# Trailing means moved to GpSimd, decayed values taken from PSUM, and another order of fills in a triangular inverse

## What is computed

```
x = x + 0.5 * swiglu(rms(x));  h = rms(x);  proj = h @ w_in            # 3080 columns
aq, ak, av, pu, dq, dk, dv, dz, db, da = split(proj)
ya = dilated_attention(rope(aq), rope(ak), av)       # 4 heads x 64
yb = pool_w_g( mean of the last w positions of pu_g - pu_g ) * scale   # w = 2, 4, 8, 16; 4 groups x 64
yc = rms(delta_rule(q, k, v, decay, beta)) * silu(dz)  # 4 heads x 128, after a causal conv of 4 taps
x = x + concat(ya, yb, yc) @ w_out;  x = x + 0.5 * swiglu(rms(x))
```

## Time and profile before

| what | value |
|---|---|
| three runs, median | 1019.83 us |
| profiled execution, its own time | 1020.79 us |
| its span, first to last instruction | 1019.0 us |
| granted TensorE clock, mean | 0.998 |
| mixer of layer 0, inverse up to the new values | 264.5 to 288.4 us |

### The profile page before, as it was taken

How to read it: one execution, slowest core, us unless ns; L and a number is a source line. 1 busy time by engine, 2 the same in 40 slices (tenths; PEclk the granted TensorE clock), 3 DMA queues, 4 the chain that set the end, 5 groups by cost and what they waited for, 6 DMA issues and landing times.

```text
span 1019.0 us, 19068 instructions
## 1 busy us (share of the span) xinstructions
PE 1007.4 (99%) x6482; PEld 883.7 (87%) x6482; DVE 726.7 (71%) x1204; ACT 602.6 (59%) x1101; POOL 235.7 (23%) x248
## 2 busy tenths in 40 slices
PE   9999999999999999999999999999999999999996
PEld 7888888899988888888888888889999888888885
DVE  5787666899777866666786666668986877666666
ACT  6555555777665655555675555558675575555554
POOL 2767222100400122222202222220014002222221
PEclk9999999999999999999999999999999999999999
DMA  7966666485224666666637666656832238666651
GB/s 232 285 209 200 190 194 192 126 242 160 75 64 124 189 206 191 195 188 187 205 123 226 188 191 193 191 157 169 228 110 64 87 101 269 196 190 190 189 182 41
DMA packets 249882, 176.79 MB, mean 173 GB/s; under 512 B 5876, under 2 KB 235401, under 8 KB 249705
## 3 DMA queue, kind: packets, MB, share of 16 engines
q1 hardware_dynamic: 248800, 174.35, 56.7%
q0 software_dynamic: 400, 1.43, 0.4%
q10 hardware_dynamic: 632, 0.34, 0.1%
HBM read 175.05 MB, written 1.05 MB: 173 GB/s over the span
## 4 chain that ended last, share of the span: by engine, by line
PE 92%; DVE 5%; ACT 2%; issue 0%; DVEq 0%; POOL 0%; POOLq 0%; ACTq 0%
PE bank L768 26%; PE bank L772 14%; PE bank L739 13%; PE bank L740 13%; PE bank L741 13%; PE bank L755 3%; PE bank L758 1%; PE bank L779 1%; DVE Wl L1887 1%; PE bank L1169 1%; PE bank L1156 1%; PE bank L1092 1%; ACT X L1491 0%; DVE X L1929 0%; PE bank L814 0%
## 5 line engine op out<-in xcount | busy, mean ns | idle before, releaser
L1887 DVE TENSOR_TENSOR Wl<-raw,Wh 128x1024 fp32r<-128x1024 f32 x324 | 401.7, 1263 | 52.9 <-ACT Wh L1420 52.7
L1420 ACT ACTIVATE Wh<-raw 128x1024 fp32r<-128x1024 f32 x323 | 322.1, 1047 | 20.7 <-PE bank L741 18.3
L768 PE MATMUL bank<-X,Wh 128*128 128x512 f32 x1216 | 288.3, 389 | 0.0
L768 PEld LDWEIGHTS bank<-X,Wh 128*128 128x128 f32 x1216 | 228.0, 188 | 47.2
L622 POOL TENSOR_TENSOR gact<-gact,pooled 128x256 f32<-128x256 f32 x85 | 63.6, 748 | 569.2 <-DVE gact L1986 559.7
L772 PEld LDWEIGHTS bank<-X,Wl 128*128 128x128 f32 x1216 | 153.9, 189 | 5.8
L772 PE MATMUL bank<-X,Wl 128*128 128x256 f32 x1216 | 155.8, 281 | 0.0
L739 PE MATMUL bank<-Wh,aH 128*128 128x512 f32 x336 | 132.4, 394 | 0.2
L740 PE MATMUL bank<-Wl,aH 128*128 128x512 f32 x336 | 131.8, 392 | 0.0
L741 PE MATMUL bank<-Wh,aL 128*128 128x512 f32 x336 | 130.8, 389 | 0.0
L1552 ACT ACTIVATE aH<-hid 128x256 fp32r<-128x256 f32 x84 | 35.1, 418 | 148.8 <-DVE hid L2001 148.8
(11 more groups left out here) (319 smaller groups left out, 1371.3 us busy)
## 6 DMA issues: line engine op xcount, KB each, us to landing
raw<-in_ffn_w_gate SPq DMA_DIRECT2D x88, 512.0 KB, 4.6
raw<-in_ffn_w_up SPq DMA_DIRECT2D x88, 512.0 KB, 3.9
raw<-in_ffn_w_down SPq DMA_DIRECT2D x88, 512.0 KB, 3.4
raw<-in_w_in SPq DMA_DIRECT2D x48, 512.0 KB, 4.9
raw<-in_w_out SPq DMA_DIRECT2D x16, 512.0 KB, 3.6
cst<-in_consts POOLq DMA_DIRECT2D x1, 1200.0 KB, 6.4
xr<-in_x SPq DMA_DIRECT2D x2, 512.0 KB, 4.1
out_x<-big SPq DMA_DIRECT2D x3, 256.0 KB, 2.6
```

The costliest lines, as they stand in the source:

```text
L768: nc.tensor.matmul(b[:, :], piece(Wh, 3 * par + j)[:, k, :], X[:, k, :, :], start=k == 0, stop=False)
L1420: return nc.scalar.activation(Wh[:, s, 0:D_MODEL], raw[:, s, :], ACT.Copy).then_inc(hi_cast.sem, 1)
L1887: return nc.vector.tensor_tensor(low_at(s, skewed), raw[:, s, :], Wh[:, s, 0:D_MODEL].bitcast(F32), ALU.subtract).then_inc(lo_cast.sem, 1)
```

## The change

1. Pieces 21, 22, 23 become: second pool block, fourth gate block, first pool block. Each is made with channels on partitions, by `fill(first, last)`, which runs steps of these three pieces; 24 steps as before, in five groups with ends 4, 9, 14, 19, 24.
2. The four groups of pool products and the two copies of their result go. ScalarE copies each pool block from PSUM to `win_x` (`pool_raw`), and GpSimd adds shifted copies of it, seven instructions for block 1 and five for block 0, each waiting for the one before it. The constant table is 688 KB in place of 1200 KB.
3. The turns of V come after level 0, in PSUM banks 0 and 1, the turns of q and k within the half level.
4. The half level's P for c = 1 and D for c = 0 are interleaved, one product of each in turn.
5. `Vd` is formed from PSUM with beta times decay ahead of `Vn`.
6. On VectorE the copies to `DT` move ahead of the half level's negations. On ScalarE the copies of V come after level 0, and the table load after the fourth gate block's activation, which moves behind the edges.

TensorE's order after the change:

```diff
+                fill(0, FILL_ENDS[0])
                 for n in range(len(LEVELS)):
-                    fill = z_part if n < Z_LEVELS else (lambda ks: att_late(6, ks))
-                    k = 4 * (n % 2)
                     for stage in (level_p, level_d):
                         for c in range(HALVES):
                             stage(n, c)
-                    fill(range(k, k + 4))
-                for first, second, k in ((quarter_p, quarter_d, 0), (half_p, half_d, 4)):
-                    for stage in (first, second):
-                        for c in range(HALVES):
-                            stage(c)
-                    att_late(7, range(k, k + 4))
-                turn_qk()
+                    if n == 0:
+                        turn_v()
+                    else:
+                        fill(FILL_ENDS[n - 1], FILL_ENDS[n])
+                for stage in (quarter_p, quarter_d):
+                    for c in range(HALVES):
+                        stage(c)
+                fill(FILL_ENDS[3], FILL_ENDS[4])
+                half_level()
...
+                def half_level():
+                    pe.wait_ge(*d_done.at(layer, 8 + 1))
+                    for h, u in units(0):
+                        m = half_p(h, u)
                     m.then_inc(p_done.sem, 1)
+                    turn_qk(0)
+                    pe.wait_ge(*d_done.at(layer, 8 + 2))
+                    pe.wait_ge(*pm_done.at(layer, 10 + 1))
+                    pe.wait_ge(*dt_edge.at(layer, 1))
+                    for (h, u), (_, v) in zip(units(0), units(1)):
+                        p = half_p(h, v)
+                        d = half_d(h, u)
+                    p.then_inc(p_done.sem, 1)
+                    d.then_inc(dd_done.sem, 1)
+                    turn_qk(1)
+                    pe.wait_ge(*pm_done.at(layer, 10 + 2))
+                    pe.wait_ge(*dt_edge.at(layer, 2))
+                    for h, u in units(1):
+                        m = half_d(h, u)
+                    m.then_inc(dd_done.sem, 1)
...
-                pe.wait_ge(*pool_copied.at(layer, 2))
+                pe.wait_ge(*win_step.at(layer, 12))
+                pe.wait_ge(*z_act.at(layer, 4))
```

GpSimd, after the rotary products:

```diff
+                def window(op):
+                    win_count[0] += 1
+                    op.then_inc(win_step.sem, 1)
+                    pool.wait_ge(*win_step.at(layer, win_count[0]))
+                def windows(j):
+                    pool.wait_ge(*pool_x.at(layer, 2 - j))
+                    x, lower, upper = win_x[:, j, 1:], slice(0, POOL_DIM), slice(POOL_DIM, P)
+                    a, b = win_a[:, 8:], win_b[:, 4:]
+                    share = cst[:, C_POOL + j * SEQ:C_POOL + (j + 1) * SEQ]
+                    window(nc.gpsimd.tensor_tensor(a, x, win_x[:, j, 0:SEQ], ALU.add))
+                    rows = upper if j == 0 else slice(0, P)
+                    window(nc.gpsimd.tensor_tensor(b[rows, :], a[rows, :], win_a[rows, 6:6 + SEQ], ALU.add))
+                    if j == 1:
+                        window(nc.gpsimd.tensor_tensor(a, b, win_b[:, 0:SEQ], ALU.add))
+                        window(nc.gpsimd.tensor_tensor(b[upper, :], a[upper, :], win_a[upper, 0:SEQ], ALU.add))
+                    window(nc.gpsimd.tensor_tensor(pooled[lower, j, :], a[lower, :], share[lower, :], ALU.mult))
+                    window(nc.gpsimd.tensor_tensor(pooled[upper, j, :], b[upper, :], share[upper, :], ALU.mult))
+                    window(nc.gpsimd.tensor_tensor(pooled[:, j, :], pooled[:, j, :], x, ALU.subtract))
...
+                windows(1)
+                windows(0)
                 ffn(layer, 1)
```

VectorE:

```diff
-                for c in range(HALVES):
-                    dve.wait_ge(*p_done.at(layer, 10 + c + 1))
-                    nc.vector.tensor_scalar(PM[HALF:, 4 * c:4 * c + 4, 0:HALF],
-                                            bank[4 + c][HALF:, 0:4 * HALF].rearrange("p (u t) -> p u t", u=4), -1.0, None,
-                                            ALU.mult).then_inc(pm_done.sem, 1)
                 dve.wait_ge(*cleared.at(layer, 1))
                 for c in range(HALVES):
                     u = slice(4 * c, 4 * c + 4)
                     dve.wait_ge(*dt_edge.at(layer, c + 1))
                     for q in BLOCKS:
                         op = nc.vector.tensor_copy(DT[q, u, q], T64[q, u, :])
                     op.then_inc(dt_joined.sem, 1)
+                for c in range(HALVES):
+                    dve.wait_ge(*p_done.at(layer, 10 + c + 1))
+                    nc.vector.tensor_scalar(PM[HALF:, 4 * c:4 * c + 4, 0:HALF], ...
                 lo_mix(layer, 26)
                 lo_mix(layer, 27)
...
+                small(nc.vector.tensor_tensor(beta_dec, beta_k[:, 0:4], dec[:, 0:4, P - 1:P].rearrange("p u t -> p (u t)"),
+                                              ALU.mult))
+                dve.wait_ge(*vn_ps.at(layer, 1))
+                nc.vector.tensor_tensor(Vd, bank[4][:, :].rearrange("p (u d) -> p u d", u=4),
+                                        beta_dec.unsqueeze(2).broadcast_to([P, 4, P]), ALU.mult).then_inc(vd_done.sem, 1)
                 new_values(0)
-                dve.wait_ge(*vn_done.at(layer, 1))
-                nc.vector.tensor_tensor(Vd, Vn[:, 0:4, :], dec[:, 0:4, P - 1:P].broadcast_to([P, 4, P]),
-                                        ALU.mult).then_inc(vd_done.sem, 1)
```

More of the change, by code:

```diff
@@ L1106, in mixer, with turn_qk @@
                 pe.wait_ge(*at_done.at(layer, 4))
-                def turn_qk():
+                def turn_qk(j):
                     pe.wait_ge(*roped.at(layer, 4))
-                    for j in range(2):
-                        for c in range(HALVES):
[L1113 to L1124, removed]
-                                  k == 0, k == KT - 1)
[L1126 to L1140, removed]
+                    pe.wait_ge(*v_copied.at(layer, j + 1))
@@ new lines, in turn_qk, with fill @@
+                    for c in range(HALVES):
+                        for pair in range(2):
+                            m = nc.tensor.transpose(bank[j][:, pair * SEQ + c * P:pair * SEQ + (c + 1) * P],
+                                                    qkr[:, c, j * 256 + pair * P:j * 256 + (pair + 1) * P], ident)
+                    m.then_inc(qk_turned.sem, 1)
+                def fill(first, last):
+                    for step in range(first, last):
+                        n, k = divmod(step, KT)
+                        pos, out = FILL_POSITIONS[n], bank[(3, 2, 3)[n]][:, 0:SEQ]
+                        s = MIX_SLOTS[pos]
+                        if step == first or k == 0:
+                            split(pos)
+                            if pos == POS_POOL1:
+                                pe.wait_ge(*diff_done.at(layer, 2))
+                            elif pos == POS_Z3:
+                                pe.wait_ge(*z_act.at(layer, 3))
+                            else:
+                                pe.wait_ge(*pool_x.at(layer, 1))
+                        m = three(out, piece(Wh, s)[:, k, :], low_piece(s)[:, k, :], Xh[:, k, :], Xl[:, k, :],
+                                  k == 0, k == KT - 1)
+                        if k == KT - 1:
+                            m.then_inc(proj.sem, 1)
@@ L1195, in quarter_d, with half_p @@
                     m.then_inc(dd_done.sem, 1)
[L1197 to L1202, removed]
-                    m.then_inc(p_done.sem, 1)
[L1205 to L1211, removed]
+                def half_p(h, u):
+                    return nc.tensor.matmul(bank[4 + u // DN_HEADS][HALF:, h * HALF:(h + 1) * HALF], LT[0:HALF, u, HALF:],
+                                            D64[0:HALF, u, :], start=True, stop=True)
@@ L1817, in mixer @@
                                      ACT.Copy).then_inc(o_done.sem, 1)
-                for j in range(2):
-                    act.wait_ge(*pool_ps.at(layer, j + 1))
-                    nc.scalar.activation(pooled[:, j, :], bank[2 + j][:, 0:SEQ], ACT.Copy).then_inc(pool_copied.sem, 1)
                 out_stats(0)
```

144 lines of the change are left out of this document (70 added, 74 removed).

## The result

The changed kernel takes 1021.66 us (median of 20 executions), the kernel before 1020.08 in the same rounds: a ratio of 1.0017, 95% interval 1.0011 to 1.0023. It is slower by 1.6 us, clear of the noise and just under 0.2%. The forecast was 1023.2 us, +3.4; sign and mechanism held, the size was about half. (One slow execution of the 20 took more than twice the time of the rest; medians and ratio don't hang on it.)

A forecast was written before the change was run, and what follows sets the result against it. TensorE, busy 1007.4 of 1019.0 us, was taken as the bound. State product +1.7 us per layer, twice, is 3.4: 1020.79 becomes 1024.2, or 1023.2 against the median 1019.83; range 1017.3 to 1024.5 (8 in 10).

The forecast's parts named there:

- timetable without GpSimd: Both mixers, inverse to state product, nothing held by GpSimd: state product at 290.45 against 291.73, -1.28 us per layer.
- The mechanism of the forecast: Inverse's end to Vd: VectorE's copies, casts and small product take turns with GpSimd's windows; state product +1.7 us per layer.
- C: The forecast itself: copies and casts held by GpSimd's windows, state product late, 1022.0 to 1024.3 us; chance 0.50.
- rival B: Half level to Vd: casts held but not copies; -0.3 to +0.2 us per layer, 1019.6 to 1020.2; chance 0.22.
- Rival A: Half level to Vd: VectorE and GpSimd hardly hold each other; -1.28 us per layer, 1017.3, or 1017.0; chance 0.20.
- D: Besides C, windows reach past 299 and the pooled product waits: 1 to 3 us per layer, 1025 to 1029; chance 0.08.
- the lower bound: State product's delay if the casts catch the gaps in GpSimd's work: +1.1 us per layer, where +1.7 was forecast.
- the wide range that reaches into A: Whole kernel's time, for 8 chances in 10: 1017.3 to 1024.5 us.
- the band "within": Whole kernel, a change under the measurable 0.2% (2.0 us): rival B and what of A and C falls short; chance 0.27.

## Why the prediction was right, and where its size was off

**TensorE's own work: right.** The timetable without GpSimd (-1.28 a layer, 1017.3) was measured as 1017.41 without windows. The inverse's levels take 4.07, the pair 0.61 (0.55 forecast).

**The mechanism of the forecast: right.** VectorE's two-input casts, the small product and the copies are held beside GpSimd. Of the copies no row of before spoke; they take 2.14 for 1.21, and 2.59 in the kernel before with windows added. This was the point between C and rival B. The Trainium skill (SBUF — State Buffer, "SBUF: two separate sides") has the fp32 copy in SBUF run in a two-port mode, and gives that mode and instructions with two SBUF inputs a lock that GpSimd shares. This case's traces agree, by these copies and by Vd: with one input from PSUM it takes 0.69 beside GpSimd, with both from SBUF 1.17. Rival A is refuted by L2325, D by the absence of any wait at the pooled product.

**The size: three terms were too large.** (1) The first block's windows: 0.82 a step, 5.7 in all, taken from the earlier trace rows. The adds take 0.61 with a step of 0.69, and the seven took 5.14. (2) The copies: forecast from 283.8 to 286.65, 2.85 us; measured 2.14 from 283.9. The wait before the pair was 0.54, not 1.15, and the new values started at 288.39, not 288.95. (3) Negation 1 to the end of Vd: forecast 5.1 (cast 26 behind one window, cast 27 behind another, the small product behind a third); measured 286.92 to 291.21, 4.3. The casts together were held by 0.57, less than one window. State product at 292.14, not 293.45: +0.41 a layer, where the lower bound was +1.1. By size that is nearer to rival B (up to +0.2) than to C. (B's lower end is added up wrongly: -0.3 a layer is 1019.2, not 1019.6.)

The common fault: where instructions met I charged nearly a whole GpSimd instruction. Measured, four copies beside L719 and L720 lost 0.93, not 1.6, and two casts 0.57, not 1.1. The first cast (1.26) was hardly held, since it started just before a window ended; only the second (1.75) met a whole one.

**What the sum missed:** 0.7 us that the medians have and the stages don't. It has no term in the forecast. It is luck that it has the forecast's sign: the median (+1.6) lies nearer to +3.4 than the stages (+0.86) do.

**How far the forecast held.** 1021.66 lies under C's own range, 1022.0 to 1024.3, and only the wide range that reaches into A holds it. It also lies less than the 2.0 us that the prediction called measurable above 1019.83, so in the band "within", which had 0.27; with 20 executions on each side the interval is finer than that, and shows the sign.

**Forecast signs against the trace:** copies 0.6 to 1.0 each (0.54 in the mean, 0.29 to 0.81 singly); 1.1 before the pair (0.54); windows between 280 and 293, three or more over 1.2 (280.4 to 292.0, two); 2 to 2.6 for Vd (1.73); no pool products (so).

## What to carry to other kernels

Work given to an idle GpSimd is paid for on VectorE, in the instructions that have two inputs in SBUF or are fast SBUF copies; before moving it, list which of these stand between a TensorE result and what TensorE waits for, and move them or feed them from PSUM. An edit's worth depends on what covers it: in the kernel before, Vd from PSUM gave nothing, and windows beside the copies cost 0.3 us in the stages. Once the pool products were gone, the one was worth about 2 us and the other cost 3.3 in the stages, there with the casts held too. Two waits on one queue don't add up: mending the earlier one alone made the kernel 2.6 us slower, about 1.6 of it in VectorE's queue.

## What the runs showed of the hardware

TensorE's clock can fall to its lower level around a short idle stretch, and only in some executions. In the version with only the order mended, TensorE had nothing to do from 288.8 to 291.8; it then ran at half its clock, 1.2 GHz, for over 3 us while busy. Its granted clock by microsecond (columns: stretch, length, PE busy, PEclk, DMA share, GB/s), and its rows:

```profile
291.00:292.00 1.00, 0.16 (x1) 0.80 0.45 131
292.00:293.00 1.00, 1.00 (x5) 0.50 0.96 349
293.00:294.00 1.00, 1.00 (x7) 0.50 1.04 324
294.00:295.00 1.00, 1.00 (x7) 0.50 1.14 342
295.00:296.00 1.00, 1.00 (x11) 0.99 1.13 335
```
```profile
291.84 2.04 PE L1348 MATMUL bank<-early 128*128 128x128 f32 x8 [3.02 <-DVE early L2385]
293.67 1.70 PE L1353 MATMUL bank<-four 128*128 128x128 f32 x8
```

From the state product's start to the products with the state, two groups on, is 3.37 us, where the changed kernel takes 1.86 (291.36 to 293.22): 1.5 us lost. In the same execution mixer 1 had as long a wait and kept its clock; in the version with the old order both mixers lost it. The version with only the casts moved showed such a spell in mixer 0, with 1.2 us of idle time ahead of the pair; it set in about 2 us after TensorE was at work again. In all, the profiled executions have twelve waits of 1.2 to 3.2 us in their mixers, and a spell by four of them; in the mixers without such a wait the granted clock stays at 1.00. So such a wait cost up to 1.5 us on top of itself in some executions, and in the version whose wait was filled with products that nothing reads, none of 11 executions was among the +3 us ones. Idle time as the cause rests on these few places; why one execution falls and another doesn't stays open.

GpSimd's adds of 128x256 take 0.61 us, and the same line on 64 partitions (L714 of the first pool block) 0.61 too: half the partitions save nothing. Products of 64x256 take 0.72 to 0.74.
